# The first pair of chunks of two block-matrix products: from four plain block products to seven products of sums

## The reference

```
# first block, MLP_HIDDEN = 4096
h = rmsnorm(x, norm_mlp[layer])
x = x + jnp.square(jax.nn.relu(h @ w_up[layer])) @ w_down[layer]
...
# second block, D_FF = 2816
def swiglu(n, w_ffn_in, w_ffn_out):
    g, u = jnp.split(n @ w_ffn_in, 2, axis=-1)
    return (jax.nn.silu(g) * u) @ w_ffn_out
```

## Time and profile before

| what | value |
|---|---|
| median of 3 runs | 954.12 us (953.78 to 954.59) |
| the profiled execution's own time | 954.2 us |
| its span, first to last instruction | 952.3 us |
| mean granted TensorE clock | 0.998 of full speed |
| PE busy | 944.3 us, 99% of the span |
| DVE, ACT, POOL busy | 700.1, 557.7, 126.8 us |

### The profile page before, as it was taken

How to read it: one execution, slowest core, us unless ns; L and a number is a source line. 1 busy time by engine, 2 the same in 40 slices (tenths; PEclk the granted TensorE clock), 3 DMA queues, 4 the chain that set the end, 5 groups by cost and what they waited for, 6 DMA issues and landing times.

```text
span 952.3 us, 16938 instructions
## 1 busy us (share of the span) xinstructions
PE 944.3 (99%) x6872; PEld 867.2 (91%) x6872; DVE 700.1 (74%) x932; ACT 557.7 (59%) x850; POOL 126.8 (13%) x178
## 2 busy tenths in 40 slices
PE   9999999999999999999999999999999999999997
PEld 7877889989999999989987999998998899999996
DVE  6768775777777887888866787786667467777777
ACT  6577545557566666566865674545455445555544
POOL 3000001004222320304000001100000012121210
PEclk9999999999999999999999999999999999999999
DMA  9974437555566666556465365555655346565661
GB/s 309 306 241 128 126 102 189 165 178 181 185 192 197 198 185 209 175 168 199 142 192 158 109 185 192 164 190 168 199 164 166 122 156 200 175 202 176 201 197 67
DMA packets 133549, 170.43 MB, mean 179 GB/s; under 512 B 5824, under 2 KB 97296, under 8 KB 133472
## 3 DMA queue, kind: packets, MB, share of 16 engines
q1 hardware_dynamic: 131408, 165.07, 55.2%
q10 hardware_dynamic: 1424, 2.84, 0.8%
q0 software_dynamic: 640, 1.44, 0.6%
HBM read 168.28 MB, written 1.05 MB: 178 GB/s over the span
## 4 chain that ended last, share of the span: by engine, by line
PE 98%; DVE 1%; issue 0%; ACT 0%; POOL 0%; POOLq 0%; ACTq 0%
PE ps L399 15%; PE ps L400 15%; PE ps L401 15%; PE ps L430 8%; PE ps L432 8%; PE ps L431 8%; PE ps L760 6%; PE ps L382 5%; PE ps L486 3%; PE ps L802 3%; PE ps L803 3%; PE ps L804 3%; PE ps L517 1%; PE ps L518 1%; PE ps L519 1%; PE ps L652 1%
## 5 line engine op out<-in xcount | busy, mean ns | idle before, releaser
L1652 DVE TENSOR_TENSOR parts<-raws,parts 128x1024 fp32r<-128x1024 f32 (+3 forms) x307 | 364.5, 1202 | 130.1 <-ACT parts L1107 129.0
L1107 ACT ACTIVATE parts<-raws 128x1024 fp32r<-128x1024 f32 (+3 forms) x307 | 309.8, 1031 | 129.8 <-PE ps L401 52.7
L399 PE MATMUL ps<-room_r,parts 128*128 128x256 f32 x1248 | 351.3, 282 | 0.0
L400 PE MATMUL ps<-room_r,parts 128*128 128x256 f32 x1248 | 348.8, 280 | 0.0
L401 PE MATMUL ps<-room_r,parts 128*128 128x256 f32 x1248 | 348.4, 279 | 0.0
L399 PEld LDWEIGHTS ps<-room_r,parts 128*128 128x128 f32 x1248 | 234.6, 188 | 2.2 <-issue 0.8
L400 PEld LDWEIGHTS ps<-room_r,parts 128*128 128x128 f32 x1248 | 234.6, 188 | 1.1
L401 PEld LDWEIGHTS ps<-room_r,parts 128*128 128x128 f32 x1248 | 234.8, 188 | 0.0
L430 PE MATMUL ps<-parts,room_r 128*128 128x512 f32 (+1 forms) x336 | 133.9, 399 | 0.7 <-DVE parts L1652 0.7
L432 PE MATMUL ps<-parts,room_r 128*128 128x512 f32 (+1 forms) x336 | 131.0, 390 | 0.0
L431 PE MATMUL ps<-parts,room_r 128*128 128x512 f32 (+1 forms) x336 | 131.0, 390 | 0.0
(11 more groups left out here) (239 smaller groups left out, 1112.8 us busy)
## 6 DMA issues: line engine op xcount, KB each, us to landing
raws<-in_w_in SPq DMA_DIRECT2D x99, 512.0 KB, 4.5
raws<-in_w_ffn_in SPq DMA_DIRECT2D x44, 512.0 KB, 4.5
raws<-in_w_up SPq DMA_DIRECT2D x32, 512.0 KB, 3.9
raws<-in_w_down SPq DMA_DIRECT2D x32, 512.0 KB, 3.7
raws<-in_w_ffn_out SPq DMA_DIRECT2D x22, 512.0 KB, 4.5
raws<-in_w_xkv SPq DMA_DIRECT2D x16, 512.0 KB, 4.0
raws<-in_w_out SPq DMA_DIRECT2D x8, 512.0 KB, 4.3
raws<-in_w_up_ssd SPq DMA_DIRECT2D x8, 512.0 KB, 4.7
```

The costliest lines, as they stand in the source:

```text
L399: e.matmul(ps, wh, hT[0][:, k, :], start=k == 0, stop=False)
L400: e.matmul(ps, wh, hT[1][:, k, :], start=False, stop=False)
L1107: e.activation(t.h, t.raw, ACT.Copy).then_inc(s["hi"], 1)
L1652: e.tensor_tensor(t.l, t.raw, t.h.bitcast(F32), ALU.subtract).then_inc(s["lo"], 1)
```

## The change

`by_sums` becomes pairs 0 to 13 of the MLP and 0 to 9 of the gated stage, so that `down(0, 0)` is done by seven products in both. Three edits follow from it. The first product into each of the two output banks now begins the accumulation there. The upper left block of the second output bank, which no product writes, is begun by the first plain pair after the products (pair 14, pair 10); its first matmul is split into two of 256 columns. In the MLP, for q = 1 and 2, ACT's rounding of the sums of pair q - 1 and DVE's rest of them stand behind the work on `up(q)`, not ahead of it; in the gated stage they stand ahead of the work on gate q for every q.

```
-        by_sums = [range(1, 14), range(1, 10)]
+        by_sums = [range(14), range(10)]
...
                     product(p1, u11, w11, first)
-                    product(c11, u12, w21)
+                    product(c11, u12, w21, first)
...
-                    sums.release = done(product(c21, u22, t4))
+                    sums.release = done(product(c21, u22, t4, first))
...
-                            e.matmul(ps, uh[:, k, tok], wh, start=q == 0 and k == 0, stop=False)
+                            if h == 0 and t and k == 0 and q == by_sums[u][-1] + 1:
+                                for c in (slice(0, 256), slice(256, 512)):
+                                    e.matmul(ps[:, c], uh[:, k, tok], wh[:, c], start=False, stop=False)
+                            else:
+                                e.matmul(ps, uh[:, k, tok], wh, start=q == 0 and k == 0, stop=False)
...
             def up(q):
                 until(where["up", q].at)
-                sums_rounded(0, q - 1)
+                if q > 2:
+                    sums_rounded(0, q - 1)
...
                 e.activation(ups[q % 4][0], r, ACT.Copy).then_inc(s["up_hi"], 1)
+                if q in (1, 2):
+                    sums_rounded(0, q - 1)
```

More of the change, by code:

```diff
@@ L2042, in vector @@
                 until(where[name].at)
-                sums_rest(0, q - 1)
+                if q > 2:
+                    sums_rest(0, q - 1)
                 full(name)
```

## The result

The changed kernel takes 956.59 us (median of 11 runs, 956.18 to 958.03), the kernel before on the same chip 954.40 us: a ratio of 1.0027, with an interval of 1.0019 to 1.0035. So it is slower by 2.2 us, as the prediction said.

The account below looks back on a forecast made before the run. PE, busy 944.3 of 952.3 us, was taken as the bound. Saving and two PE waits, -0.64 + 2.62 + 0.47 = +2.45, on the profiled 954.2 gave 956.65; the median lying 0.08 lower, 956.6 was forecast, range 954.3 to 958.2.

Parts of the forecast that it names:

- The saving: First pair of each stage: 21 matmuls in 2.48 us replace twelve in 2.80, 0.32 us saved each, 0.64 in all.
- The MLP does not wait: MLP: operands come in time, tightest at up(3)'s second tile with 1.7 us of room; rival that it waits: 957.5 to 958.5, 0.05.
- The chain in the gated stage: Gated stage: hidden sums make gate 1 1.71 us late on DVE; down(0, 1)'s tile is ready at 802.36, PE wants it at 799.85.
- the long 3.21 us: Gated stage: POOL's three additions and handing over to ACT take 3.21 us, the long value against 2.60 in the MLP.
- the short wait: Rival, gated stage: POOL and DVE do not slow each other, down(0, 1)'s tile comes at 801.4; 955.1 to 956.0 us, chance 0.13.
- The two waits: Gated stage: PE waits 2.51 us (2.62 with restart) ahead of down(0, 1), then 0.36 (0.47) at gate 3's second tile.
- The clock: Rival, gated stage: PE's clock falls to its lower level in the first wait; 957.2 to 958.2 us, chance 0.20.

Follow-up runs that it names:

- the MLP alone: Kernel before with pair 0 done by seven products in the MLP only, the gated stage as before: 955.36 us, ratio 1.0007.
- the gated stage alone: Kernel before with pair 0 done by seven products in the gated stage only, the MLP as before: 959.65 us, ratio 1.0055.
- sums_behind: Changed kernel with hidden sums of pairs 0 and 1 put behind the next pair's work in the gated stage: 956.04 us, ratio 1.0014.
- the tile early: Changed kernel with one tile more made ahead of gate 2 and of prod 2 on ACT and DVE: 956.00 us, ratio 1.0014.
- with both: Changed kernel with the edits of sums_behind and the tile early together: 954.77 us, ratio 1.0002.
- the further tile at pair 3: The kernel with both edits, and a tile made one place earlier at pair 3 as well: 954.02 us, ratio 0.9993.
- before_moved: Kernel before with an unused ten-column buffer that shifts the buffers behind it by 64 bytes, no instruction added: 966.39 us, measured once.

## Why the prediction was right

**The saving.** 0.32 us a pair was forecast and is there: 2.48 us for 21 matmuls in both stages.

**The MLP does not wait.** Right, in this kernel and with the MLP alone; its saving reaches the time (0.55 us by the medians, though the interval of the ratio takes in 1) once the fetch is out of the way.

**The chain in the gated stage.** The steps hold one by one, counted from prod 0 on DVE: gate 1 at 5.26 forecast and 5.25 measured, gate 2 at 16.85 and 16.87, the rest of the tile of down(0, 1) at 19.24 and 19.25. POOL needed the long 3.21 us (782.32 to 785.53), so the mechanism of the short wait was not there: that rival wanted the tile's rest to end by 801.8, 19.91 behind prod 0, and it ended at 802.03, 20.48 behind it.

**The two waits.** The first was forecast at 2.51 us and is 2.30; the second at 0.36 + 0.11 and is 0.38 + 0.10. The term that was off is the lead with which the chain starts: PE's pair began 15.75 us behind prod 0 and not 15.48 (so, relative to PE, gate 1 is 1.43 us later and not 1.7). PE did not come later; prod 0 came earlier. It ends a string of work on ACT and DVE that begins with the rounding of a weight tile, and that rounding waits for the tile's transfer. It is 5.49 us ahead of prod 0 in both kernels:

```profile
776.40 1.07 ACT L1107 ACTIVATE parts<-raws 128x1024 fp32r<-128x1024 f32 x1 [0.48 <-DMA raws<-in_w_ffn_in]
...
776.06 1.06 ACT L1111 ACTIVATE parts<-raws 128x1024 fp32r<-128x1024 f32 x1 [0.92 <-DMA raws<-in_w_ffn_in]
```

The first row is of the kernel before, the second of the changed one. The rounding came 0.34 us earlier, PE's pair only 0.07. So the landing of one transfer sets how long PE waits. In the six traces with the change in the gated stage the pair begins 15.44 to 16.11 us behind prod 0; by the 18.05 us that are left when the 2.48 of the products are taken from 20.53 (prod 0 to PE's restart), the first wait would lie between 1.9 and 2.6 us, which is an estimate. With the gated stage alone the distance is 15.52, and the wait of 2.54 fits it:

```profile
776.90 1.06 ACT L1111 ACTIVATE parts<-raws 128x1024 fp32r<-128x1024 f32 x1 [0.63 <-DMA raws<-in_w_ffn_in]
...
782.38 0.69 DVE L1693 TENSOR_TENSOR room<-ps,room 128x512 f32<-128x512 f32 x1 [2.11 <-ACT room L1609]
...
797.91 2.65 PE L760 MATMUL ps<-parts,room_r 128*128 128x256 f32 x21
```

The 16.11 is that of sums_behind. At 15.5 PE would stand 0.6 us longer there, which would take its profiled 955.31 to about the median; that is argued, since each kernel has one trace.

The sum by this trace is -0.64 + 2.30 + 0.10 + 0.48 = +2.24, against +2.45 forecast and +2.19 by the medians. That the forecast of 956.6 and the median of 956.59 agree to 0.01 us is luck: the sum was 0.2 too long, the profiled execution lost 0.35 in its first microseconds (its first pair of the MLP begins at 230.66, where the plain one began at 230.31), and the median of the kernel before lies between 954.12 and 954.79 from one comparison to the next.

**What was behind the wait.** That hidden sums and the tile's place add up was the prediction's chain, and the four runs show it. Against the kernel before, the change stands at +2.2 us, with the sums behind +1.4, with the tile early +1.2, with both +0.1, and with the further tile at pair 3 -0.8. It is a lateness of two engines that is handed from tile to tile, not one late tile.

**The clock.** It did not fall in the profiled execution: both windows of PE's timeline around the wait have 1.00.

```profile
797.00:802.00 5.00, 2.95 (x25) 2.74 (x24) 3.29 (x5) 2.69 (x4) 0.00 (x0) 1.00 0.35 108
802.00:807.00 5.00, 4.70 (x26) 3.96 (x27) 3.98 (x6) 3.14 (x4) 3.00 (x3) 1.00 0.63 192
```

But it is close. With the gated stage alone PE stood 2.54 us and the clock fell; here it stood 2.30 and it did not; the 0.24 us between them are the 0.23 by which the leads of their chains differ, 15.75 and 15.52. Of the eleven runs, four have a mean clock of 0.996 or 0.997 and took 957.45 to 958.03 us, where that rival had 957.2 to 958.2; the other seven have 0.998 and took 956.18 to 957.51, six of them under 956.6. The difference in the mean, 0.0015 of 955 us, is 2.9 us at half the clock, near the 3.4 us seen with the gated stage alone. Where it fell in those four was not recorded, so that it was in this wait is argued, not shown. The Trainium skill, page "TensorE: Matmul & The Clock Gate", section "HAM oscillation — how this bites in real kernels", says that a wait between bursts can send the clock to its lower level; the kernel of which it says so has longer waits than these. The run with the gated stage alone agrees, with 0.50 behind the wait.

**What the prediction did not have.** The end of the kernel, by which a change of ten instructions on engines off the path can cost 0.9 us. In the changed kernel it happens to be nothing (6.54 us to the end, as before), but it is part of why the expectations for one stage at a time were off: without it 955.36 would have been about 954.4, and 959.65 about 958.7, an estimate from the 0.93 us by which their ends are longer. Nor did it have the landing of the weight tile, by which the wait differs from one trace to the next.

## What to carry to other kernels

Where two engines hand work to each other in written order, follow the lateness, not the wait: moving one item only moves the wait to the next tile, until the tiles behind it come in time as well. Count from a common event (here prod 0): along the chain of ACT and DVE the distances came out within 0.02 us of the forecast, while the absolute times shift by some tenths. Then ask what that event itself waits for, since its distance to the engine that asks may differ from one trace to the next, here by 0.7 us. For changes under 1 us, compare the last matmul as well as the span, and where the two disagree look at the transfers behind it.

## What the runs showed of the hardware

- Instructions come by DMA packets on queues of their own; those of q14 have 8 KB (0.19 MB in 23 packets in the kernel before). One that falls among the last packets of the output made the end 0.9 us later, in four kernels (7.46 to 7.48 us behind the last matmul, against 6.53 to 6.56 in the others).
- Moving small buffers and the rooms by 64 bytes made the kernel 12 us slower. PE's timeline of before_moved, at two pairs by sums of the MLP:

```profile
255.61 2.63 PE L761 MATMUL ps<-parts,room_r 128*128 128x256 f32 x21
266.64 2.66 PE L761 MATMUL ps<-parts,room_r 128*128 128x256 f32 x21
```

From pair to pair it is 11.03 us, against 10.89 in the kernel before (241.50 to 252.39), with no wait of PE in either:

```profile
252.39 2.65 PE L760 MATMUL ps<-parts,room_r 128*128 128x256 f32 x21
```

The loss is in the matmuls that stream their columns from the buffer that moved. From start to start the 3744 matmuls of L399 to L401, which stream from `room_r`, take 2 to 3.5 ns more each, 10.2 us in all; those of L760, which stream from `parts`, which did not move, take 118 ns in both kernels. What in the address does it stays open; it was not tried further.
- PE's granted clock fell from 2.4 to 1.2 GHz in a wait of 2.54 us amid a stream of matmuls, and stayed there for some 3.4 us.
